# Expert stage of a two-layer encoder: the next pair's gate and up products ahead of the current pair's down products

## The reference, cut to what matters

```
e_idx  = two experts of the best group, for each token          # 32 experts in all
hid    = silu(x @ w_gate[e]) * (x @ w_up[e])                    # 1024 -> 256
y      = hid @ w_down[e]                                        # 256 -> 1024
x      = x + gate_0 * y_0 + gate_1 * y_1
```

## Time and profile before

| what | value |
|---|---|
| median of 3 runs | 1279.36 us (1279.34 to 1279.62) |
| the profiled execution's own time | 1279.65 us |
| its span, first to last instruction | 1278.0 us |
| PE busy | 1063.3 us, 83% |
| DVE, ACT, POOL busy | 493.3, 289.6, 272.5 us |
| expert stage of layer 0 | about 401 to 666 us of the span |
| expert stage of layer 1 | about 971 to 1250 us of the span |
| moved by DMA | 303.67 MB, mean 238 GB/s |

### The profile page before, as it was taken

One profiled execution on the slowest core, in us unless ns is written; L12 is line 12 of the kernel. 1 busy time (PEld: TensorE's weight loads), 2 busy tenths in 40 slices (PEclk: granted clock), 3 DMA queues, 4 the chain that ended last, 5 costly groups with the idle time before them and its releaser, 6 DMA issues.

```text
span 1278.0 us, 14398 instructions
## 1 busy us (share of the span) xinstructions
PE 1063.3 (83%) x5242; PEld 609.9 (48%) x5242; DVE 493.3 (39%) x1066; ACT 289.6 (23%) x616; POOL 272.5 (21%) x289
## 2 busy tenths in 40 slices
PE   6999999998995978887854999987985978788870
PEld 5777777774543333332323777743543323333320
DVE  3234444344356111110116699993455111111116
ACT  3233232333111101000003455553111100000002
POOL 3000000000003111111042488850003111101033
PEclk9999999999995999988885999998996989999895
DMA  8953322302706999999955922100027999999963
GB/s 278 389 172 109 109 97 78 106 22 105 296 36 227 408 419 420 420 420 421 414 174 132 367 61 66 33 25 0 34 101 286 413 421 421 421 420 420 379 255 131
DMA packets 107791, 303.67 MB, mean 238 GB/s; under 512 B 18248, under 2 KB 65480, under 8 KB 82745
## 3 DMA queue, kind: packets, MB, share of 16 engines
q1 hardware_dynamic: 85481, 254.74, 51.4%
q0 software_dynamic: 22256, 48.22, 10.4%
HBM read 278.34 MB, written 57.12 MB: 262 GB/s over the span
## 4 chain that ended last, share of the span: by engine, by line
PE 58%; DMA 21%; DVE 10%; issue 8%; ACT 2%; SPq 1%; POOL 0%; DVEq 0%; POOLq 0%
DMA ring<-in_w_up 16%; PE bank L1200 12%; PE bank L522 10%; PE bank L421 7%; PE bank L1217 6%; PE bank L549 4%; DVE bank L1680 2%; PE bank L1478 2%; PE bank L572 2%; PE bank L1190 2%; PE bank L588 2%; PE bank L613 2%; PE bank L346 2%; DMA work<-in_w_pw 1%; PE bank L954 1%
## 5 line engine op out<-in xcount | busy, mean ns | idle before, releaser
L1200 PE MATMUL bank<-ring,work 128*64 128x512 f32 x704 | 179.1, 667 | 34.9 <-DMA ring<-in_w_up 33.1
L1217 PE MATMUL bank<-ring,work 128*64 128x512 f32 x528 | 124.9, 616 | 36.7 <-DVE work L1236 22.4
L1478 PE MATMUL bank<-arena,work 128*128 128x288 f32 x512 | 129.2, 415 | 8.2 <-issue 3.2
L1200 PEld LDWEIGHTS bank<-ring,work 128*64 128x64 f32 x704 | 61.4, 153 | 150.3 <-issue 147.8
L522 PE MATMUL bank<-arena,ring 128*128 128x288 f32 x512 | 131.9, 412 | 0.0
L1232 DVE TENSOR_TENSOR work<-work,bank 128x256 f32<-128x256 f32 x33 | 13.9, 421 | 292.2 <-ACT work L1228 292.2
L1478 PEld LDWEIGHTS bank<-arena,work 128*128 128x128 f32 x512 | 99.0, 195 | 38.0 <-issue 8.3
L1627 POOL TENSOR_TENSOR ring<-ring 128x606 f32<-128x606 f32 x76 | 103.8, 1365 | 55.8 <-ACT ring L1576 46.2
L522 PEld LDWEIGHTS bank<-arena,ring 128*128 128x128 f32 x512 | 94.9, 190 | 32.6 <-issue 7.9
L421 PE MATMUL bank<-ring,arena 128*128 128x512 f32 x224 | 100.9, 604 | 6.6 <-ACT arena L1611 6.6
L1680 DVE SCALAR_TENSOR_TENSOR bank<-work,ring,bank 128x606 f32<-128x606 f32 x129 | 98.8, 844 | 0.0
(11 more groups left out here) (256 smaller groups left out, 1293.9 us busy)
## 6 DMA issues: line engine op xcount, KB each, us to landing
ring<-in_w_down SPq DMA_DIRECT2D x32, 2048.0 KB, 24.1
ring<-in_w_gate SPq DMA_DIRECT2D x22, 2048.0 KB, 22.0
ring<-in_w_up SPq DMA_DIRECT2D x22, 2048.0 KB, 28.9
arena<-in_w_gate SPq DMA_DIRECT2D x10, 2048.0 KB, 23.0
arena<-in_w_up SPq DMA_DIRECT2D x10, 2048.0 KB, 31.1
ring<-in_w_qkv SPq DMA_DIRECT2D x24, 512.0 KB, 6.0
y_sorted<-gain POOLq DMA_DIRECT2D x8, 1536.0 KB, 5.7
work<-in_w_pw SPq DMA_DIRECT2D x16, 512.0 KB, 5.1
```

The lines of the kernel that those rows point to most:

```text
L1200: mm = nc.tensor.matmul(bank[2 + s][rr, :], xte[s][:, c, rr], wgu[g][:, :, e, c, :], start=c == 0, stop=c == C - 1)
L1217: mm = nc.tensor.matmul(bank[5 + h][rr, :], hts[:, c, rr], wdn[s][:, e, c, h * HALF:(h + 1) * HALF], start=c == 0, stop=c == FC - 1)
L1478: mm = nc.tensor.matmul(bank[banks[h][w]][:, 0:GT], wp[s][:, w, c, :], xt[:, c, h * GT:(h + 1) * GT], start=c == 0, stop=c == C - 1)
```

## The change

On PE, ACT and DVE the loop is shifted: the up products of pair i+1 and the turn of the rows of pair i+2 come before the down products of pair i. With `local` 0 both pairs' up products come first. POOL gathers rows three pairs ahead instead of two, behind the turn of pair i+1. SP's list, the buffers and the data are as before. The whole diff:

```
-                if local + 2 < EPAIRS:
+                if local == 0:
                     pool.wait_ge(base.xt_mm, i + 1)
-                    rows_in(local + 2)
+                    rows_in(2)
+                if local + 3 < EPAIRS:
+                    pool.wait_ge(base.xt_mm, i + 2)
+                    rows_in(local + 3)
                 if local < 2 * TILES - FAR_FIRST:
                     far_rows(*far[FAR_FIRST + local])
...
             def body(i, s, k, local, more):
-                ex_up_pe(pe, base, i, s, *gu_slot(l, local))
+                if local == 0:
+                    ex_up_pe(pe, base, i, s, *gu_slot(l, local))
+                    ex_turn_pe(pe, base, i + 1, 1 - s, k)
                 if more:
-                    ex_turn_pe(pe, base, i + 1, (s + 1) % 2, k + (s + 1) // 2)
+                    ex_up_pe(pe, base, i + 1, 1 - s, *gu_slot(l, local + 1))
+                if local + 2 < EPAIRS:
+                    ex_turn_pe(pe, base, i + 2, s, k + 1)
                 ex_down_pe(pe, base, i, s, k, 1)
...
             def body(i, s, k, local, more):
-                ex_silu_act(act, base, i, s)
+                if local == 0:
+                    ex_silu_act(act, base, i, s)
+                    ex_turn_copy(act, nc.scalar.copy, base, i + 1, 1 - s, 0, base.xt_ev_a)
                 if more:
-                    ex_turn_copy(act, nc.scalar.copy, base, i + 1, (s + 1) % 2, 0, base.xt_ev_a)
+                    ex_silu_act(act, base, i + 1, 1 - s)
+                if local + 2 < EPAIRS:
+                    ex_turn_copy(act, nc.scalar.copy, base, i + 2, s, 0, base.xt_ev_a)
                 ex_y_copy(act, nc.scalar.copy, base, i, s, k, 0, base.y_ev_a)
...
             def body(i, s, k, local, more):
-                ex_hid_dve(dve, base, i, s)
+                if local == 0:
+                    ex_hid_dve(dve, base, i, s)
+                    ex_turn_copy(dve, nc.vector.tensor_copy, base, i + 1, 1 - s, 1, base.xt_ev_d)
+                if local + 2 < EPAIRS:
+                    ex_turn_copy(dve, nc.vector.tensor_copy, base, i + 2, s, 1, base.xt_ev_d)
+                ex_ht_dve(dve, base, i)
                 if more:
-                    ex_turn_copy(dve, nc.vector.tensor_copy, base, i + 1, (s + 1) % 2, 1, base.xt_ev_d)
-                ex_ht_dve(dve, base, i)
+                    ex_hid_dve(dve, base, i + 1, 1 - s)
                 ex_y_copy(dve, nc.vector.tensor_copy, base, i, s, k, 1, base.y_ev_d)
```

## The result

| | before | after |
|---|---|---|
| median | 1279.49 us (1279.34 to 1282.82, 4 runs) | 1321.45 us (1320.22 to 1326.98, 4 runs) |
| ratio, 95% interval | | 1.033 (1.0296 to 1.0364) |
| span of the profiled execution | 1278.0 us | 1318.9 us |
| last up products of pair 15, layer 0 / layer 1 | 647.16 / 1215.71 | 652.67 / 1245.56 |
| late gathers begin, layer 0 | 666.14 | 684.25 |

Slower, as forecast, but by 42 us where 24.6 were forecast, and 1.45 us beyond the upper end of the range. In the code after, the lines of the products have moved: L1193, L1203, L1210, L1220, L1247 are the old L1190, L1200, L1207, L1217, L1244; the gathers are L1166 and SP's loads L1348 and L1352.

What follows compares the result with a forecast made beforehand. The weight stream was taken to pace the expert stages past the first half dozen pairs, with PE following. 1279.65 + 4 (stream) + 10.8 (end of layer 0) + 9.9 (end of layer 1) = 1304.3, median 1304.0 us; range 1292 to 1320.

Steps and rivals of the forecast that it cites:

- Part 1: PE loop: the 2.20 us between up and down products stay, nothing leaves a turn; gain 0.
- Part 2: Weight stream: later releases let the queue run dry once per two loop links; +4 us, bounds -1 and +18 to +27.
- the slow case: Weight stream: landing to release with slow up products (9.49 instead of 7.10 us) takes 15.4 us, with quick ones 13.0.
- the 2.6 of the row: Weight stream: load latency, 7.6 us for a load alone, of which 5.0 are transfer, so 2.6.
- Part 3: First pairs: down weights 2 issued about 8.7 us later, covered by backlog; 0 in layer 0, at most a microsecond in layer 1.
- Part 4: Row gathers on POOL: same distance and number, 16 a layer; cost 0.
- Part 5: End of layer 0: scatter 15 waits behind down 14 and early gathers, 661.49 to 672.3; +10.8 us, bounds +3.8 and +12.
- Part 6: End of layer 1: overflow loads issued later, its up products move from 1232.17 to 1242; +9.9 us, bounds +6.4 and +14.
- The dry queue: Rival, weight stream: queue runs dry by more, +18 to +27 instead of +4, giving 1318 to 1327; chance 0.17.
- The lagging engines: Rival, stream's end: shallow queue evens the ragged end, last gate/up up to 10 us earlier per layer, 1284; chance 0.07.
- PE as the bound: Rival, up products: the 45.2 us of weight waits shrink, 1255 if all go, 1270 if two thirds; chance 0.03.
- The hidden ends: Rival, layer ends: early gathers and overflow loads cost nothing beyond down 14 (4 and 6 us), 1290; chance 0.07.

Runs made afterwards that it cites:

- Experiment 8: Changed kernel with gate/up first in SP's list, three early gathers ahead of scatter 15, overflow gate/up loads issued earlier: 1281.75 us, ratio 1.0023 to the kernel before.
- Experiment 1: Kernel before, SP alone altered: from `local` 3 on it waits for the down products of one pair later before issuing loads; 1317.82 us, ratio 1.0299.
- experiment 3: Kernel before, SP alone altered: waits for the down products of one pair later, but only from `local` 6 on; 1295.83 us, ratio 1.0153.
- experiment 7: Changed kernel, SP alone altered: overflow rows, gate and up weights wait for pair 14's turn and up products, only down weights for down 14; 1317.89 us.
- experiments 6: Changed kernel, POOL alone altered: three early gathers stay ahead of scatter 15, five go behind it; 1316.75 us, ratio 1.0296 to the kernel before.

## Why the prediction was right or wrong

*Part 1, the PE loop: right.* In the changed kernel nothing is gained in a turn: 13.0 us from the start of the up products to the release in the quick turns (546.28 to 559.27), as before. Experiment 8 confirms it from the other side.

*Part 2, the stream: right in mechanism, wrong in size, and this made the miss.* +4 was forecast, +16.8 came. That the queue runs dry at one release in two, and that the pace is then the mean of loop and stream, held. The step that failed is the term built on it: 0.4 us a pair, charged to half of the pairs.

In layer 0 the releases at 508.94, 544.98, 579.84 and 614.50 find the queue empty or short of work. From landing to release it was 14.4 to 15.9 us ahead of them, mean 15.0, where 15.4 was taken for the slow case. From release to the next landing it was 19.7 to 21.9, mean 20.4, where 2.6 + 17.15 = 19.75 was taken. The loop is so 15.0 + 20.4 - 17.15 = 18.3 us instead of 18.0, and its mean with 17.15 is 17.7, which is the pace measured (17.73). Three sizes were wrong:

- The slow share. The forecast had half of the products slow. In the loop with these releases every one was (8.5 to 10.0 us, behind 3.4 to 7.5 us of waiting; the granted clock was 0.70 over the ten microseconds from 529.08, and 1.00 over the 7.09 from 546.28). The mean already shares one slow loop between two pairs, so 0.4 a pair was due for all pairs: 0.2 too little.
- The pace of before. It was taken from SP's issues, 17.15. From up products to up products it was 16.95 in layer 0 and 16.56 in layer 1: 0.2 and 0.6 too little.
- The loop itself, 18.3 instead of 18.0: 0.15 too little. What the longer way from release to landing is made of isn't settled; the start after an empty queue (DMA share 0.04 and 0.87 in two neighbouring microseconds) is part of it.

With the 0.2 that was forecast this is 0.75 a pair in layer 0, where 0.8 was measured, and 1.15 in layer 1, where it was 1.4. The rest in layer 1 stays open in its size; there two releases in a row, 1170.81 and 1190.09, found the queue short of work (DMA share 0.59 and 0.08 in their microseconds).

The range failed at the same term. Part 2 names +18 to +27 as its upper bound, but the sum for the range puts in +10. With +18 it would have reached 1322 and held the result.

The weighing against the Trainium skill's fixed cost ("DMA: Bandwidth & Descriptors", anatomy of one DMA) came out against the lower figure: it would have made the term +1. That section gives its about 2.0 us for DMAs issued from GpSimd, and these loads are issued by SP. In the loop above, release to landing less 17.15 us is 3.3 us, more than the page's figure and more than the 2.6 of the row.

*Part 3, first pairs: right.* DMA share 0.98 at 400 GB/s from 434 to 509, and the up products of pair 7 start at 510.79 against 511.58 before. Experiment 1 shows what an uncovered ramp costs: it is 22 us over experiment 3, 11 a layer.

*Part 4, gathers of rows: right.* No up product or turn waits for them in the chain of the changed kernel.

*Part 5, end of layer 0: right.* From up 15 to scatter 15 +10.6 us where +10.8 was forecast. Missed: 2.0 us because the scatter lands more slowly than before.

*Part 6, end of layer 1: right.* From up 15 to the overflow's up products 26.0 us, forecast 26.3 (its +9.9 is 9.8 by its own rows, 1242 - 1232.17). Missed: 2.0 us because they then run 9.11 us. The windows view gives the granted clock of their first 4 us as 0.50, the lower of the engine's two levels (1.2 and 2.4 GHz), after 8 us in which PE had almost nothing to do; in experiment 7, with no idle time ahead, the clock is 1.00 and the same products take 7.09.

```profile
1263.40:1271.50 8.10, 1.10 (x10) 0.91 (x8) 1.38 (x2) 1.17 (x2) 6.27 (x7) 0.84 1.00 396
1271.50:1275.50 4.00, 3.94 (x10) 1.24 (x12) 0.00 (x0) 0.00 (x0) 1.11 (x2) 0.50 1.02 416
```

*The rivals.* The dry queue, given 0.17 and 1318 to 1327, got the time and the place, though at +17 and not +18 to +27: the forecast with +16.8 in place of +4 is 1316.8, and only the two misses at the ends bring it into the rival's span. That its number was met is so in part luck. By its own condition, landing-to-issue plus latency more than 2 us over 17.15, it wasn't the case: that sum was 18.3, 1.2 over. The lagging engines did not catch up enough to give anything back. PE as the bound is not borne out: in experiment 8 the stream is full again and the time is that of the kernel before. The hidden ends are refuted by experiments 6 and 7.

## What to carry to other kernels

When work is moved ahead of a step that releases a buffer, count the queue in time: what is still queued at the landing that PE waits for, against the time from that landing to the next release, with the products at the duration that they have behind a wait. If the two are within a few microseconds of each other, take the loss as real. The cheap repair is on the issuing side: a buffer that the new order frees earlier must also be the one that the issuing engine refills first. And a software pipeline shifted by one step adds its step to the end of the loop, where everything that was hidden behind the last transfer (gathers, overflow loads) has lost its cover.

## What the runs showed that was not expected

- The price of a later release isn't proportional to it: releases 7 to 10 us after the landing cost 2.1 us in sum (ratio 1.0018), those 13 to 16 us after it, and that from `local` 6 on alone, cost 16.8.
- With the queue shallow the ragged end of the stream shrinks: DMA share 0.59 in the last 5 us before up 15 of layer 0, where it was 0.23. The last landing came no earlier for it (652.67 against 647.16), so nothing is gained.

```profile
647.00:652.00 5.00, 3.65 (x16) 1.05 (x16) 1.57 (x4) 0.81 (x2) 0.00 (x0) 1.00 0.59 246
```
